# Latent attention: third group's turned probabilities evicted ahead of the last exponentials, last gate and output pieces around the last turn and values

## The reference

```python
z, xbc, dt_raw, q_a, c_kv, k_rope, gate_ssd, gate_mla = split_cols(u @ w_in[i], IN_SPLITS)
y_ssd = ssd_branch(...) @ w_ssd_out[i]
y_mla = mla_branch(q_a, c_kv, k_rope, positions, ...) @ w_mla_out[i]
merged = jax.nn.sigmoid(gate_ssd) * y_ssd + jax.nn.sigmoid(gate_mla) * y_mla
h = h + merged @ w_o[i]
h = h + memory_cross_attention(rms_norm(h, norm_xattn[i]), rms_norm(mem, norm_mem[i]), w_xq[i], w_xkv[i], w_xo[i])
h = h + hierarchical_moe(...)

# in mla_branch, per block of 128 queries
sc = jnp.where(kpos[None, :] <= qpos[:, None], einsum('bqhd,bkhd->bhqk', qi, k) * scale, -jnp.inf)
pr = jax.nn.softmax(sc, axis=-1)
o = jnp.einsum('bhqk,bkhd->bqhd', pr, v)
```

## Time and profile before

| | |
|---|---|
| median of 3 runs | 1092.04 us (1090.55 to 1095.19) |
| profiled execution, its own time | 1089.01 us |
| its span, first to last instruction | 1087.2 us, mean granted clock 0.981 |
| PE busy | 1011.7 us, 93% of the span |
| DVE, ACT, POOL busy | 621.3, 517.4, 19.4 us |
| chain that ended last | PE 69%, DMA 11%, DVE 11%, ACT 6% |

### The profile page before, as it was taken

The page is one execution under the profiler, slowest core; times in us unless marked ns, Lnnn a source line. Parts: engine busy times, 40 slices in busy tenths (PEclk is TensorE's granted clock), DMA queues, the critical chain, the costliest instruction groups (busy, mean ns, idle before and its releaser), DMA issues.

```text
span 1087.2 us, 19436 instructions
## 1 busy us (share of the span) xinstructions
PE 1011.7 (93%) x8574; PEld 932.8 (86%) x8574; DVE 621.3 (57%) x828; ACT 517.4 (48%) x701; POOL 19.4 (2%) x24
## 2 busy tenths in 40 slices
PE   7999989899999999999997768699999999999998
PEld 6999878799889999998765545389999999999998
DVE  6798677765565893544111110079994765555566
ACT  5576577745556573542211110168567563443453
POOL 0000020001000000000000000000000000000000
PEclk9999999999999999998999888899999999999999
DMA  7666342346224456499999999775320366555431
GB/s 280 249 221 228 117 188 91 148 166 233 78 78 162 171 197 251 168 387 381 412 420 420 422 419 421 310 294 194 127 107 34 132 232 210 183 190 194 169 141 40
DMA packets 34872, 240.97 MB, mean 222 GB/s; under 512 B 4064, under 2 KB 4448, under 8 KB 6368
## 3 DMA queue, kind: packets, MB, share of 16 engines
q1 hardware_dynamic: 33264, 232.54, 56.0%
q0 software_dynamic: 1232, 6.99, 1.7%
q10 hardware_dynamic: 288, 0.15, 0.1%
HBM read 238.58 MB, written 1.08 MB: 220 GB/s over the span
## 4 chain that ended last, share of the span: by engine, by line
PE 69%; DMA 11%; DVE 11%; ACT 6%; issue 2%; SPq 1%; DVEq 0%; ACTq 0%
PE ps L462 16%; PE ps L463 16%; PE ps L464 16%; DMA wr<-in_c_weights 8%; DVE wlo L1976 4%; PE ps L535 3%; PE ps L1225 3%; DMA T<-in_c_weights 2%; ACT whi L1324 2%; PE ps L1191 1%; PE ps L928 1%; DMA raw<-in_c_weights 1%; SPq L2945 1%; PE ps L1252 1%; PE ps L1265 1%
## 5 line engine op out<-in xcount | busy, mean ns | idle before, releaser
L1976 DVE TENSOR_TENSOR wlo<-raw,whi 128x2048 fp32r<-128x2048 f32 (+1 forms) x119 | 269.4, 2267 | 134.2 <-ACT whi L1324 134.0
L462 PE MATMUL ps<-XUh,whi 128*128 128x256 f32 x992 | 280.8, 283 | 8.6 <-DVE wlo L1976 7.7
L463 PE MATMUL ps<-XUl,whi 128*128 128x256 f32 x992 | 276.9, 279 | 0.0
L464 PE MATMUL ps<-XUh,wlo 128*128 128x256 f32 x992 | 276.9, 279 | 0.0
L1324 ACT ACTIVATE whi<-raw 128x2048 fp32r<-128x2048 f32 (+1 forms) x119 | 223.5, 1882 | 64.0 <-PE ps L464 61.6
L462 PEld LDWEIGHTS ps<-XUh,whi 128*128 128x128 f32 x992 | 188.6, 190 | 10.7 <-issue 8.3
L463 PEld LDWEIGHTS ps<-XUl,whi 128*128 128x128 f32 x992 | 187.4, 189 | 0.3
L464 PEld LDWEIGHTS ps<-XUh,wlo 128*128 128x128 f32 x992 | 187.0, 189 | 0.0
L1225 PE MATMUL ps<-wr,Xg 128*32 128x256 f32 x480 | 55.2, 455 | 20.1 <-DMA wr<-in_c_weights 10.9
L2867 DVE SCALAR_TENSOR_TENSOR sphs<-sphs,wsl,ps 128x256 f32<-128x256 f32 x8 | 3.8, 481 | 94.7 <-ACT sphs L1941 94.7
L1225 PEld LDWEIGHTS ps<-wr,Xg 128*32 128x32 f32 x480 | 29.2, 130 | 32.4 <-issue 28.6
(11 more groups left out here) (621 smaller groups left out, 2368.7 us busy)
## 6 DMA issues: line engine op xcount, KB each, us to landing
raw<-in_c_weights SPq DMA_DIRECT2D x139, 1024.0 KB, 4.9
wr<-in_c_weights SPq DMA_DIRECT2D x36, 1024.0 KB, 26.3
xhi<-in_c_weights SPq DMA_DIRECT2D x12, 1024.0 KB, 26.0
xlo<-in_c_weights SPq DMA_DIRECT2D x12, 1024.0 KB, 26.4
extra<-in_c_weights SPq DMA_DIRECT2D x10, 1024.0 KB, 27.4
acb<-sums POOLq DMA_DIRECT2D x4, 1024.0 KB, 4.7
T<-in_c_weights SPq DMA_DIRECT2D x4, 1024.0 KB, 24.8
T8b<-in_c_weights SPq DMA_DIRECT2D x4, 1024.0 KB, 26.0
```

The lines of the kernel that those rows point to most:

```text
L462: pe.matmul(ps, h(k), xh(k), start=start and k == 0, stop=False, skip_group_check=loose)
L463: pe.matmul(ps, h(k), xl(k), start=False, stop=False, skip_group_check=loose)
L464: t = pe.matmul(ps, l(k), xh(k), start=False, stop=stop and k == kt - 1, skip_group_check=loose)
L1976: dve.tensor_tensor(l[:, 0:n], r, h[:, 0:n].bitcast(F32), ALU.subtract).then_inc(*did("w_lo", "split", i))
```

## The change

In PE's program gate piece 3 is moved ahead of turn 3. Output pieces 0 and 1 form one `chunks_late` with late = 6, and the values of group 3 are called inside it, after the first part of piece 0. In ACT's program the exponentials of group 3 are moved behind the values of group 1 and the eviction of group 2's turned probabilities; gate piece 3 is moved ahead of the eviction of group 3's turned probabilities; the sigmoid (with its table load) is moved ahead of the values of group 3. The programs of DVE, POOL and SP are as before. The banks change hands in the new order of PE.

```diff
@@ -477,7 +477,7 @@
                            lambda k: xh[:, k, :], lambda k: xl[:, k, :], kt, ready)
             t.then_inc(*did("w_used", "used", i))
 
-        def chunks_late(name, cs, xh, xl, kt, ready, late):
+        def chunks_late(name, cs, xh, xl, kt, ready, late, between=None):
 
             pss = {}
             for part in (range(late), range(late, kt)):
@@ -497,6 +497,8 @@
                             t = pe.matmul(d, l[:, k, f], xh[:, k, :], start=False, stop=k == kt - 1, skip_group_check=True)
                     if kt - 1 in part:
                         t.then_inc(*did("w_used", "used", i))
+                    elif c == cs[0] and between is not None:
+                        between()
 
         def chunk_tok(name, c, xh, xl, kt, ready, banks=bank):
             i = first[name] + c
@@ -769,11 +771,10 @@
         mla_turn(2)
         gate_mla(2)
         mla_values(2)
+        gate_mla(3)
         mla_turn(3)
-        gate_mla(3)
-        mla_values(3)
-        chunks_late("mla_out", (0,), OAh, OAl, 8, lambda k: at_("emptied", "o", k // 2), 6)
-        for c in range(1, 4):
+        chunks_late("mla_out", (0, 1), OAh, OAl, 8, lambda k: at_("emptied", "o", k // 2), 6, between=lambda: mla_values(3))
+        for c in range(2, 4):
             chunk("mla_out", c, OAh, OAl, 8, lambda k: at_("emptied", "o", k // 2))
 
 
@@ -1608,17 +1609,17 @@
         values(0)
         gate_mla(1)
         turned_p(1)
-        soft(3)
         values(1)
         turned_p(2)
+        soft(3)
         gate_mla(2)
         values(2)
+        gate_mla(3)
         turned_p(3)
-        gate_mla(3)
-        values(3)
         table(SIGM)
         w.wait_ge(*at_("emptied", "gate_mla", 3))
         act.activation(G2[:, :, :], G2[:, :, :], ACT.Sigmoid).then_inc(*did("mix_act", "mix", "sig2"))
+        values(3)
         for c in range(4):
             upcoming("mla_out", c)
             w.wait_ge(*at_("mix", "sum", c))
```

## The result

The changed kernel took 1082.32 us (median of 8 runs, 1080.93 to 1087.63) against 1092.03 of the kernel before (median of 8 runs, 1086.20 to 1095.19): a ratio of 0.9923, interval 0.9899 to 0.9947. The forecast was 1091.6 with a range of 1088.6 to 1094.4, so the time lies outside it. The profiled execution took 1084.42, its span is 1082.6 us, the mean granted clock 0.978, and PE is busy 1007.8 us. Lines behind the edit are one or two further down than before (DVE's L2377 is L2378, PE's L751 is L753).

A forecast was written before the change was run, and what follows sets the result against it. The loop of DVE and ACT, not PE, was taken to decide when `w_o` finishes, leaving 0.46 us of PE's 2.5 us stall as gain: 1092.04 - 0.46 = 1091.6 us, range 1088.6 to 1094.4.

The forecast's parts named there:

- The stretch: From gate piece 1 to PE's first product with the memory, wait at 384.05: forecast to gain 0.46 us.
- PE's wait ahead of values 2: PE's 2.5 us stall for the turned probabilities on ACT, ending at 327.31: claimed to vanish.
- exponentials of group 3: ACT's last exponentials at 321.62: not delayed by the evictions put ahead, as DVE's maxima arrive then; cover 0.7 us.
- first product, against before: DVE's first product with the gate, starting the output loop: at 344.97 instead of 345.18, only 0.2 us earlier.
- turn of the loop: DVE and ACT handing output pieces to each other from 345.18 on: 6.12 us a turn, as before.
- new waits of PE at `w_o`: PE, ahead of schedule at `w_o`, waits 1.05 us for the third lower half and 0.5 for a split.
- The upper bound: Output pieces at 0.1133 us a matmul would start the loop 0.8 us earlier, for a gain of 1.05.
- The slower rival: Late closing of output piece 0 with PE's stall remaining: first product 2.3 us later, total 1094.3; chance 0.12.
- The full 2.5 us of the stall: Rival that the output loop is looser than read and the whole gain stays: 1089.5 us; chance 0.12.
- the size of a matmul: Streams show 0.112 to 0.113 or 0.118 us a matmul; each stream was assumed to keep its profiled pace.
- The rival that named this: Another pace downstream: the stream at 888.90 at 0.113 gives back 6.4 us, 1085.2, or others slow, 1093; chance 0.10.

The follow-up runs named there:

- e2: The changed kernel with ACT's last exponentials put back in their old place: 1092.16 us against 1088.32 of the kernel before, ratio 1.0036.
- e1: Only ACT's last exponentials moved, behind values 1 and the eviction of turned probabilities 2, in the kernel before: 1084.91 us against 1088.32, ratio 0.9963.
- e16: ACT's part alone with two constant matmuls at each of five places inside the last long stream: one run, 1092.33 us.
- e4: The kernel before, unchanged, run once more for its profile: one run, 1091.41 us.
- e8: ACT's part alone with twelve constant matmuls ahead of PE's wait before the last long stream: 1086.19 us against 1089.72 of the kernel before, ratio 0.9985.
- e5: ACT's part alone with one constant matmul between PE's wait and the last long stream: 1082.86 us against 1089.72 of the kernel before, ratio 0.9971.
- e7: ACT's part alone with four constant matmuls between PE's wait and the last long stream: 1083.00 us against 1089.72 of the kernel before, ratio 0.9953.
- e6: ACT's part alone with two constant matmuls between PE's wait and the last long stream: 1082.10 us against 1089.72 of the kernel before, ratio 0.9957.
- e14: ACT's part alone with two constant matmuls ahead of the last long stream, measured again: 1084.97 us against 1085.73 of the kernel before, ratio 0.9991.
- e15: The kernel before with two constant matmuls ahead of the last long stream: 1085.12 us against 1085.73 of the kernel before, ratio 0.9987.

## Why the prediction was wrong, point by point

**The stretch: right, step for step.** Counted from gate piece 1, to take out where each execution began:

| | predicted | measured |
|---|---|---|
| PE's wait ahead of values 2 | gone | gone |
| exponentials of group 3 | not delayed | not delayed, ACT idle 0.57 ahead of them |
| first product, against before | 0.2 earlier | 0.14 earlier (41.04 against 41.18) |
| turn of the loop | 6.12 | 6.13 |
| new waits of PE at `w_o` | 1.05 and 0.5 | 1.00 and 0.49 |
| whole stretch | 0.46 gained | 0.44, 0.54, 0.54 gained (three profiles) |

That the first profile gives 0.44 beside the forecast 0.46 is closer than the working deserves. Gate piece 3 ran at 0.3533 us per group in all four profiles of kernels that move it (the changed kernel's three and e2), where the prediction kept 0.3400; in the other order it had 0.3400 in 13 of 14 profiles. That costs 0.2 us on 16 groups. The first 36 matmuls of output piece 0 ran the other way, at 0.3400 in those four profiles where the prediction kept 0.3533, which gives 0.16 back. That the two cancel is luck. The upper bound itself is too high: 84 matmuls of the output pieces stand ahead of the closing of piece 0, and 84 x 0.0045 is 0.4 us, not 0.8.

The slower rival's mechanism was right as well and was priced at 2.3 us; e2 shows it at 2.0. The full 2.5 us of the stall could not be kept, and e1 shows why: it is the closing of output piece 0 that the loop starts from, and the change delays it by 36 matmuls.

**The step that failed: the size of a matmul.** The prediction saw both paces, and then wrote "I take the paces of the rows, since code and buffers of each stream are unchanged". That was a guess, and the step that failed. Unchanged code and buffers did not keep the pace: the changed kernel ran the last stream in 157.51, 163.67 and 157.50 us in its three profiles. Over all 18 profiles the two paces came nine times each. The rival that named this priced it well (6.4 us; the first two profiles show 6.2), but gave it 0.10, and put it on the new kernel only. The profile before was itself a draw, at the slower pace, and 1092.03 was the median of runs most of which look like it (7 of 8 above 1090). The changed kernel's 8 runs had 7 of 8 below 1085. A term that each execution draws is a term of the measurement as well: with it the range had to reach 6 us down from the start, to 1085 at least. Even that would not have held the 1082.32 of the first set.

**What 9.7 us were.** With the changed kernel measured two more times the ratios are 1.0002 and 0.9994. What the profiles show of the change as such is about a microsecond: 0.5 us of the stretch in every profile, and the falls of the clock that it spares, 3 in 6 of 1.3 to 1.8 us, some 0.7 in the mean. The times can't confirm so little: both intervals reach over 2 us to either side of no change. The profile pair differs mainly by the pace of the last stream. That the rest of the difference of the medians is also made of such draws is inferred from the repeats and from the two heaps of times, as only one run of each set has a profile. One stream's pace is worth 6.2 us, so for 9.7 other draws must have fallen the same way, such as the fall near 210 us; which ones did stays open. That 7 of 8 changed runs and 1 of 8 runs before fell into the lower heap was, by the two repeats, in the main luck of the first set. Whether the change moves the odds of the draw by some path isn't settled: over its three sets 19 of 30 runs lie in the lower heap, against 26 of 60 of the kernel before beside them.

**A term that was missing.** The prediction booked the gap at its length. In half of the profiles that have it, it is followed by some 3 us at 1.2 GHz. The Trainium skill (TensorE: Matmul & The Clock Gate, "Why this matters for your kernels") asks for no long idle gaps of PE between bursts of matmuls, as they drop the throughput. The gap here is 2.5 us; three of six profiles agree, at 1.3, 1.3 and 1.8 us each, and three do not.

**What could have been better.** ACT's part alone gives a stretch shorter by 1.2 us and the ratios 0.9963 and 0.9982; each time its mean is under that of the kernel before (by 3.1 and 2.2 us), though the second interval holds no change. It moves one call past two others, and is better than the whole change in the stretch by 0.7 to 0.8 us.

## What to carry to other kernels

Before a stall of PE is booked as a gain, look which engine's loop follows and what starts it: here the loop of DVE and ACT (6.12 us a turn against 5.65 of PE) took back all but half a microsecond, because the same edit delayed the product that starts it. Compare stretches between two marks in the trace, not whole times, when a change is worth less than the spread of the executions. And if the times of one kernel lie in two heaps, one set of eight runs on each side can show a difference with a tight interval that the next set does not; repeat both before it is believed.

## What the runs showed of the hardware

- A long stream of 128 x 128 by 128 x 256 matmuls ran at 0.3400 or at 0.3533 us per group of three, at a granted clock of 1.00 and with PE never idle. The pace held for 472 groups, through all semaphores that were already met and through constant matmuls put between (e16, one execution). The same instructions had the other pace in another execution: 6.2 us on this stream. Some streams never changed in the 18 profiles: that from 33 to 103 us was always at 0.3400, that from 236 to 265 always at 0.3533. And at one place the pace went with the order of the program: gate piece 3 was at 0.3533 in all four profiles that move it and at 0.3400 in 13 of the 14 others (the 14th, e4, has it behind a fall of the clock). What picks the pace is open. It is there within the first three groups. Neither taking away the wait ahead of the stream (e8) nor one or four matmuls behind it (e5, e7) brought the times into one heap; for two (e6, e14, e15) it isn't settled.
- The granted clock can fall to 0.50 (1.2 GHz) about 1.3 us after PE has taken up work again behind a gap of 2.5 us, and stays there for at least 3.2 us; in other executions with the same gap it does not fall (3 of 6). Behind the wait of 2.2 to 2.5 us near 210 us it fell in 9 of 18, there from 0.3 us before to 0.7 us after PE's next matmul.
